# Attention in a decoder layer: scores recomputed with keys as weights, value matmuls with 64-column weights

## The reference

```python
smask = (kpos <= t)                       # keys of the 8 chosen 64-key blocks of each query and group
s_s = einsum('bqgrd,bgqkd->bqgrk', qb, ksel)
p_s = masked_softmax(s_s, smask)          # exp(s - max) * mask / sum
o_s = einsum('bqgrk,bgqkd->bqgrd', p_s, vsel)
wmask = (wpos >= 0) & (diff >= 0) & (diff < WINDOW)       # the last 512 keys
s_w = einsum('bqgrd,bkgd->bqgrk', qb, kwin)
p_w = masked_softmax(s_w, wmask)
o_w = einsum('bqgrk,bkgd->bqgrd', p_w, vwin)
out = g[..., 0:1] * o_cmp + g[..., 1:2] * o_sel + g[..., 2:3] * o_win
```

## Time and profile before

| | us |
|---|---|
| median of 3 runs | 1602.13 |
| lowest and highest of them | 1602.12, 1605.62 |
| the profiled execution | 1602.32 |
| its span, first to last instruction | 1600.5 |
| busy in the span: PE, PEld | 1407.8, 868.7 |
| busy in the span: DVE, ACT, POOL | 564.3, 398.4, 203.1 |

### The profile page before, as it was taken

The page is one execution under the profiler, slowest core; times in us unless marked ns, Lnnn a source line. Parts: engine busy times, 40 slices in busy tenths (PEclk is TensorE's granted clock), DMA queues, the critical chain, the costliest instruction groups (busy, mean ns, idle before and its releaser), DMA issues. The chain is left out here.

```text
span 1600.5 us, 16935 instructions
## 1 busy us (share of the span) xinstructions
PE 1407.8 (88%) x6098; PEld 868.7 (54%) x6118; DVE 564.3 (35%) x1130; ACT 398.4 (25%) x974; POOL 203.1 (13%) x250
## 2 busy tenths in 40 slices
PE   6999999999866699999995799998549999999980
PEld 2555555555445587888874455655424444444430
DVE  1323432234363357555452122444531111111115
ACT  1111111111115445544441122323101111111110
POOL 1121211122110021110000000000011111111104
PEclk9999999999987669999997999999669999999995
DMA  9311100112086211100503001110518999999938
GB/s 367 103 38 53 53 27 27 53 40 66 1 296 237 74 33 42 39 2 27 224 7 122 27 27 40 53 40 27 180 57 278 372 368 371 372 366 371 368 136 315
DMA packets 126916, 227.96 MB, mean 142 GB/s; under 512 B 6272, under 2 KB 82304, under 8 KB 126720
## 3 DMA queue, kind: packets, MB, share of 16 engines
q1 hardware_dynamic: 118640, 197.17, 35.1%
q0 software_dynamic: 7056, 25.69, 4.2%
q10 hardware_dynamic: 1152, 4.19, 0.8%
HBM read 185.09 MB, written 41.94 MB: 142 GB/s over the span
## 5 line engine op out<-in xcount | busy, mean ns | idle before, releaser
L437 PE MATMUL pj<-arena,xT 128*128 128x512 f32 (+1 forms) x768 | 315.3, 564 | 15.2 <-DMA gcol<-in_gcol 15.2
L1719 PE MATMUL egu<-arena,exT 128*128 128x512 f32 x512 | 228.1, 599 | 1.2 <-issue 1.2
L437 PEld LDWEIGHTS pj<-arena,xT 128*128 128x128 f32 x768 | 143.3, 191 | 156.7 <-issue 136.3
L1719 PEld LDWEIGHTS egu<-arena,exT 128*128 128x128 f32 x512 | 95.8, 192 | 110.7 <-issue 110.2
L1118 DVE TENSOR_REDUCE anm<-asc 128x1 f32<-128x640 f32 (+7 forms) x128 | 90.6, 708 | 124.1 <-PE asc L1022 123.4
L1079 ACT ACTIVATE ap<-asc,anm 128x640 f32<-128x640 f32 (+7 forms) x128 | 89.8, 701 | 159.6 <-DVE anm L1118 149.3
L1707 PE MATMUL eyp<-arena,ehT 128*128 128x512 f32 x256 | 115.2, 593 | 1.1 <-ACT ehT L1750 1.1
L1277 PE MATMUL xpj<-arena,xTA 128*128 128x512 f32 x256 | 112.8, 599 | 0.7 <-ACT xTA L1344 0.7
L228 ACT ACTIVATE raw<-pj,xr 128x512 f32<-128x512 f32 (+1 forms) x48 | 31.4, 655 | 300.0 <-PE pj L437 300.0
L1777 DVE TENSOR_TENSOR eh<-esg,egu 128x256 f32<-128x256 f32 x32 | 13.5, 421 | 220.7 <-ACT esg L1756 220.7
L1033 PE MATMUL atp<-early,ap 128*128 128x128 f32 x528 | 84.5, 285 | 5.1 <-ACT apT L1090 4.4
(11 more groups left out here) (317 smaller groups left out, 1940.5 us busy)
## 6 DMA issues: line engine op xcount, KB each, us to landing
arena<-in_w_gate SPq DMA_DIRECT2D x32, 1024.0 KB, 7.4
arena<-in_w_up SPq DMA_DIRECT2D x32, 1024.0 KB, 9.7
arena<-in_w_down SPq DMA_DIRECT2D x32, 1024.0 KB, 11.5
y_d<-ey SPq DMA_DIRECT2D x32, 512.0 KB, 9.6
arena<-in_w_in SPq DMA_DIRECT2D x6, 2048.0 KB, 18.2
y_d<-arena SPq DMA_DIRECT2D x2, 4096.0 KB, 18.6
x<-in_x ACTq DMA_DIRECT2D x8, 512.0 KB, 3.8
xT<-in_xT SPq DMA_DIRECT2D x8, 512.0 KB, 4.0
```

The costliest lines, as they stand in the source:

```text
L437: last = nc.tensor.matmul(dst[:, 0:n], xT[i % 2][:, k, :], w[c][:, k, :], start=k == 0, stop=k == KT - 1)
L1719: last = nc.tensor.matmul(gu[k % 2][:], xT[k % 2][:, c, :], m.gateup[k][:, c, :], start=c == 0, stop=c == KT - 1)
```

## The change

Scores are computed twice. First, only with the high part of the query and in the old orientation, for the maximum of each query, head and branch (`maximum` on TensorE, 192 pieces of at most 512 keys, two PSUM banks; VectorE reduces each). The negated maxima, and the choice of blocks, are transposed once per tile (`turn_shift`), spread over four heads in bf16 (`spread`, `shift`), and later added to the scores by a matmul with constant rows (`m.chosen`, `m.plain`), which also carries the mask of unchosen blocks.

Then the work goes by slots: `attention_slots` gives tile, branch, key tile b and group g, 132 in all. A slot's scores have the key tile as the weight and the group's four heads by 128 queries as 512 moving columns (high, low, causal or window mask if it has one, shift). They land transposed, so ScalarE's exponential writes what the value matmul needs; there are no transposes and copies of probabilities. `values` takes the two slots of a pair, with 64 columns of V as the weight and the 512 probabilities as the moving operand; group 0 goes to partitions 0 to 63 and group 1 to 64 to 127 of one bank. Denominators: GpSimd adds the key tiles' probabilities elementwise (`add`, 100 of 128x512), and `denominators` sums over partitions with matmuls whose weight is a shifted unit column. `keep` and `turn_back` bring result and denominators back to one query per partition.

The maxima of tile i+1 are spread over the slots of tile i (`share`); those of tile 0 come before the first slot. ScalarE makes the high parts, GpSimd the low ones, three buffers each, and SyncE loads the first three tiles' queries at once. The spare stores now stand ahead of the store of tile 7. `phase_select` loads 1 MB of constant rows ahead of the output weights and keeps `m.notsel`.

```diff
+def attention_slots():
+    for i in range(NT):
+        for branch, k0, n in ((0, 0, i + 1), (1, max(0, i - 4), min(i + 1, 5))):
+            for b in range(n):
+                for g in range(NG):
+                    yield i, branch, k0, b, n, g
...
@@ phase_select, sync
+                sp.dma_start(m.tail[:, 0:2 * S + 2], io["chosen"]).then_inc(s["rows_in"], 16)
                 sp.dma_start(m.w_out, io["w_out"].rearrange("(k p) n -> p k n", p=P)).then_inc(m.w_out_in, 16)
...
@@ phase_attend
+    DEN, KEEP, BACK, GATE = 2, 3, 3, 4
+    at_pair = lambda j, lag: [x for x in range(X) if last_pair[x] + lag == j]
+    def share(n):
+        i = slots[n][0]
+        k, total = n - first_slot[i], first_slot[i + 1] - first_slot[i]
+        if i + 1 == NT:
+            return range(0), False
+        use, count = max(1, total - 2), len(pieces[i + 1])
+        return range(count * min(k, use) // use, count * min(k + 1, use) // use), k == total - 1
...
@@ sync
+                for i in range(3):
+                    load_q(i)
+                load_oc(0)
+                load_oc(1)
                 for i in range(NT):
+                    if i + 3 < NT:
+                        load_q(i + 3)
                     if i == NT - 1:
                         sp.wait_ge(m.w_out_in, 48)
...
                             sp.dma_start(spare[b], m.w_out).then_inc(s["spare"], 16)
-                store(NT - 2)
-                store(NT - 1)
+                    store(i)
+                    if i + 2 < NT:
+                        load_oc(i + 2)
...
@@ tensor
+                def maximum(i, p):
...
+                    if f >= 2:
+                        pe.wait_ge(s["read"], f - 1)
...
+                    last = nc.tensor.matmul(dst[:, 0:n * P], qhi[i % 3][:, h, :], kT[:, g, (k0 + c) * P:(k0 + c + n) * P],
+                                            start=True, stop=not masks and not chosen)
...
+                def scores(n):
...
+                    if n >= 2:
+                        pe.wait_ge(s["expd"], n - 1)
+                    keys = (m.kwT if branch else m.ksT)[:, g, (k0 + b) * P:(k0 + b + 1) * P]
+                    dst = sT[n % 2]
+                    for j, q in enumerate((qhi, qlo)):
+                        nc.tensor.matmul(dst[:], keys, q[i % 3][:, 4 * g:4 * g + 4, :].rearrange("p h q -> p (h q)"),
+                                         start=j == 0, stop=False)
+                    for at, mask in marks_of(i, branch, k0, b, 1, nb):
+                        nc.tensor.matmul(dst[:], mask[:], bc(m.identb[:].unsqueeze(1), [P, 4, P]), start=False, stop=False)
...
+                    nc.tensor.matmul(dst[:], keep, shift[i % 2],
+                                     start=False, stop=True).then_inc(s["scored"], 1)
...
+                def values(j):
...
+                    for g in range(NG):
+                        at = (k0 + b) * P + g * HD
+                        last = nc.tensor.matmul(ov[branch][g * HD:(g + 1) * HD, :], v[:, at:at + HD], target(2 * j + g),
+                                                start=b == 0, stop=b == nb - 1)
...
+                def denominators(x):
...
+                    for r in range(HPG):
+                        for g in range(NG):
+                            last = nc.tensor.matmul(dn[g * HD:(g + 1) * HD, 0:P], unit[:, HPG - 1 - r:HPG - 1 - r + HD],
+                                                    acc[x % 2][g][:, r * P:(r + 1) * P], start=r == 0, stop=r == HPG - 1)
...
+                pe.wait_ge(s["ready"], 2)
+                for p in range(len(pieces[0])):
+                    maximum(0, p)
+                turn_shift(0)
+                for j in range(J + BACK):
+                    if j < J:
+                        for n in (2 * j, 2 * j + 1):
+                            scores(n)
+                            some, turning = share(n)
+                            for p in some:
+                                maximum(slots[n][0] + 1, p)
+                            if turning:
+                                turn_shift(slots[n][0] + 1)
+                    if 1 <= j <= J:
+                        values(j - 1)
+                    for x in at_pair(j, BACK):
+                        turn_back(x)
+                    for x in at_pair(j, DEN):
+                        denominators(x)
...
@@ scalar
+                    nc.scalar.activation(target(n), sT[n % 2][:], ACT.Exp).then_inc(s["expd"], 1)
...
@@ gpsimd
+                    a = acc[branch][g][:]
+                    nc.gpsimd.tensor_tensor(a, a, target(n), ALU.add).then_inc(s["summed"], 1)
```

More of the change, by code:

```diff
@@ L1037, in values @@
[L1037 to L1046 removed]
+                    dst = mx[f % 2]
+                    masks = marks_of(i, branch, k0, c, n, total)
@@ new lines, in maximum, with turn_shift @@
+                    for j, (at, mask) in enumerate(masks):
+                        last = nc.tensor.matmul(dst[:, at * P:(at + 1) * P], m.identb[:], mask[:], start=False,
+                                                stop=j == len(masks) - 1)
+                    last.then_inc(s["top"], 1)
+                def turn_shift(i):
+                    f = turn_of[i]
+                    pe.wait_ge(s["wide"], i + 1)
+                    pe.wait_ge(s["read"], f - 1)
+                    nc.tensor.transpose(mx[f % 2][:, 0:P], m.tail[:, 2048:2048 + P],
+                                        m.c("ident")).then_inc(s["top"], 1)
@@ new lines, in keep @@
+                def keep(x):
+                    act.wait_ge(s["denned"], x + 1)
+                    if x >= 2:
+                        act.wait_ge(s["turned"], x - 1)
+                    nc.scalar.activation(oT[x % 2], ov[x % 2][:], ACT.Copy).then_inc(s["kept"], 1)
+                    nc.scalar.activation(dT[x % 2], dn[:, 0:P], ACT.Copy).then_inc(s["kept"], 1)
+                for i in range(3):
+                    high(i)
+                for n in range(U + 2 * KEEP):
+                    if n % 2:
+                        for x in at_pair(n // 2, KEEP):
+                            keep(x)
+                    if n >= U:
+                        continue
+                    exponentials(n)
+                    i = slots[n][0]
+                    if n == (first_slot[i] + first_slot[i + 1]) // 2 and 3 <= i + 2 < NT:
+                        high(i + 2)
@@ L1169, in _ @@
[L1169 to L1178 removed]
+                nc.vector.memset(wide, 0.0).then_inc(s["ready"], 1)
@@ new lines, in _ @@
+                done(nc.vector.memset(unit[:], 0.0))
+                nc.vector.memset(unit[:, HPG - 1:HPG], 1.0).then_inc(s["ready"], 1)
+                dve.wait_ge(s["ready"], 2)
+                for p in range(len(pieces[0])):
+                    maximum(0, p)
+                widen(0)
+                spread(0)
+                for j in range(J + GATE + STEPS + 1):
+                    for n in (2 * j, 2 * j + 1):
+                        if n < U:
+                            i = slots[n][0] + 1
+                            some, turning = share(n)
+                            for p in some:
+                                maximum(i, p)
+                                if p == len(pieces[i]) - 1:
+                                    widen(i)
+                            if turning:
+                                spread(i)
+                        if n == 2 * j:
+                            for i, k in steps_at(j):
+                                finish(i, k)
+                            for x in at_pair(j, GATE):
+                                if x >= 2:
+                                    gate(x)
+                    for x in at_pair(j, BACK):
+                        if x < 2:
+                            gate(x)
```

374 lines of the change are left out of this document (199 added, 175 removed).

## The result

The changed kernel takes 1610.78 us (median of 20 runs, 1604.52 to 1617.79) against 1603.60 us (median of 20, 1600.46 to 1614.35) of the kernel before on the same chip: a ratio of 1.0038, 95% interval 1.0022 to 1.0053, some 6.1 us slower (the two medians alone lie 7.2 apart). Forecast was 1600, 1.9 us faster than before, in a range of 1594 to 1608. The profiled execution took 1614.64 us (span 1612.7). A few executions, whatever the kernel, fall into a second, slower state; the ratios here leave them out.

The account below looks back on a forecast made before the run. TensorE was taken to bound the attention stage (busy 239 of 248 us in its middle). Start +6.3, tile 1 to last values -10.6, end +2.4: -1.9 from 1602.3 gives 1600.4, forecast 1600, range 1594 to 1608.

Parts of the forecast that it names:

- Value pairs, overlap, the price for changing shape: A pair's two value matmuls overlap fully in column halves, 0.85 us, plus 0.33 for changing array shape: 1.2 us.
- Rivals 4 and 5: Value pairs slower: partial overlap, 1.43 us a pair, 1619, chance 0.10; no overlap, 70 us more, 1670, chance 0.05.
- Denominators: TensorE's 16 times 8 matmuls of 128 columns in alternating halves: 1.2 us each time, 19.2 us in all.
- Start: From the selection stage to tile 1's beginning at 577.7 us: a loss of 6.3 us.
- a store's wait behind 1 MB: In the selection stage, the output copy's store waits behind the constants in SyncE's queue: 2.7 us more.
- Tile 0 itself: Attention's first tile: 16 maximum pieces before any slot, 7.7 us, then its slots, three at half clock taking 5.1 us.
- From tile 1 to the last values: TensorE's stretch from 577.7 to 850.6 us: 272.9 us, against 283.5 before, a gain of 10.6.
- 6% waits: TensorE's waiting from tile 1 on, taken at the earlier kernel's share: 15.4 us, between 5 and 31.
- Rival 3: VectorE's reductions pace TensorE in bursts of maxima or behind a finishing step: waits of 31 us, 1616, chance 0.16.
- At most 1.18 each: GpSimd's 100 additions of 128x512: at most 1.18 us each, hidden; from 1.3 us they would pace the last tile.
- End: From the last values to the addition of both branches: 4.3 us, against 1.9 before, a loss of 2.4.
- 8 MB of spare stores: Stores moved behind tile 6 go out about 34 us before the last store, take 18.6 to land: hidden.

Follow-up runs that it names:

- e7: Changed kernel with both value products of a pair in the same column half from tile 1 on; 1651.65 us, one run.
- e6: Kernel before with only the changed kernel's selection stage (1 MB load and GpSimd's copies); 1.0021 of the kernel before.
- e3: Changed kernel with the 1 MB load issued behind the fourth compressed tile's store; 1.0020 of the kernel before.
- e5: Changed kernel with the edits of e1 and e2, and finish steps 5 and 6 one pair later; 0.9987 of the kernel before.
- e9: e5 with the constant rows packed as bf16 pairs and loaded in place, without GpSimd's copies; 0.9964 of the kernel before.
- e10: e9 with GpSimd's additions cut to 8 of 512 columns and the gate's inversion made a copy; 0.9883 of the kernel before.
- e1: Changed kernel with GpSimd taking the power step ahead of the additions of the same pair; 1.0044 of the kernel before.
- e2: Changed kernel with VectorE's gates ahead of its finish steps, and two buffers for the first gated sum; 1.0015 of the kernel before.
- e11: e9 with the whole additions of exponentials on VectorE instead of GpSimd; 0.9985 of the kernel before.
- e4: Changed kernel with GpSimd's additions cut to 8 of 512 columns and the gate's inversion made a copy; 0.9946 of the kernel before.

## Why the prediction was wrong

Point by point, against its own steps:

- **Value pairs, overlap, the price for changing shape.** Right: 1.01 us from the pair's first start to the next line and some 0.1 ahead of it, where 1.2 in all was forecast; e7 confirms 0.85 for the overlap. Rivals 4 and 5 are out. Denominators: 1.09 us for 16 matmuls at full clock, forecast 1.2.
- **Start.** Tile 1 was forecast to begin at 577.7 and begins at 578.95, but 3.74 us of that is scatter from upstream, so the near hit is luck. From the selection's first load on, the start costs 3.8 us more than before in this profile, not 6.3. In it the selection stage has 1.96 (3.4 by e6), where 2.7 were forecast for another reason: a store's wait behind 1 MB. The store's wait did not come, and moving the load (e3) did not help; what fits the profiles is GpSimd's copy. Tile 0 itself costs 1.9 and not 3.6; the clock was at full from 571.0 to 574.4 us, before the end of its slots, and half again until 577.8.
- **From tile 1 to the last values.** Forecast 272.9, of it 256.5 work, 15.4 waits ("I take 6% waits again, 15.4 us") and 1 for the clock. Measured 861.0 - 578.95 = 282.1, so waits and clock are 25.6 instead of 16.4. **This is the step that failed**, by 9.2 us. The work was right: TensorE is busy 259.4 us there, some 3.2 of them lost to half clock. Its waits were mis-sized: they are 22.6 us, and the 7.2 too many are the one wait of 7.0 us for the gate in tile 2, which the forecast did not have. The clock behind it is the other 2.2 (3.2 instead of 1). Without that wait (e5, whose edits aim at it) the kernel is 8.2 us faster.
- **Luck in the rest of it.** Less the 7.0 us the waits are 15.6, the forecast's 15.4 almost to the point. But no wait of the changed kernel had gone into that number, and 13 us of the run hang on additions (e9, e10) that the forecast had as hidden. The share fitted by chance.
- **Why it failed.** The waits were carried over as a share from a kernel whose queues looked different. The text named finishing steps in VectorE's queue, but priced none: neither that the power step (1.65 us) is behind two additions on GpSimd, nor that a gate stands behind a step which waits for it. Rival 3 is nearest: it named a finishing step in the queue among its places, and its mark, more than 20 us of TensorE's idle time put down to VectorE, was met with 21.6 (8.6 + 7.9 + 4.3 + 0.8). But its mechanism was pacing by the reductions, which was 7.9 us only, and its price too high (31 us of waits and 1616, against 22.6 and 1610.8).
- **GpSimd's additions.** "At most 1.18 each" was too low:

```profile
L1234 POOL TENSOR_TENSOR aacc<-aacc,kcvcT 128x512 f32<-128x512 f32 x68 | 89.1, 1329 | 96.0 <-PE aov L1132 73.9 <-ACT kcvcT L1194 21.8
```

  1.33 us is over the 1.3 named as the point where they pace the last tile; they did not (GpSimd 32.87 of 40 us busy, TensorE 39.94). Their cost is of another kind, and the forecast had it at nothing, as hidden: 13 us by e9 and e10.
- **End.** Last values to addition of the branches 865.36 - 861.0 = 4.4, forecast 4.3. From the last store to the next stage's first load it is 3.15 us instead of 2.40. The forecast had the 8 MB of spare stores as hidden, going out 34 us before the last store; they went out 21.7 us before it (850.70 and 872.35 us). The traces show that they hold the next stage: in the changed kernel, e1, e2, e3, e5, e9 and e11 its first load comes 24.7 to 24.9 us behind them, whenever the last store goes, while in e4, e7 and e10, where the last store is 23.4 us or more behind them, the step after it is 2.40 to 2.42 us.

Sum of the profile: +1.96 selection, +1.85 start, -1.4 from tile 1, +2.5 end, +0.5 behind it (from that addition to the next stage's first load 10.1 us, before 9.6), 5.4 us; the runs say 6.1.

The groups of VectorE's operations by shape, 577 to 862 us of the changed kernel, show who is slowed (busy us, mean ns):

```profile
L1291 DVE TENSOR_TENSOR arena<-atp,aw 128x512 f32<-128x512 f32 x15 | 10.4, 692 | 0.5
L1307 DVE TENSOR_TENSOR arena<-arena 128x512 f32<-128x512 f32 x7 | 9.8, 1397 | 0.2
L1290 DVE TENSOR_TENSOR aw<-aw,gate 128x8 f32<-128x8 f32 x15 | 9.0, 597 | 0.5
...
L1311 DVE TENSOR_REDUCE astat<-arena 128x8 f32<-128x512 f32 x7 | 4.7, 678 | 0.1
```

Operations on two tiles in SBUF are slowed (in the mean, L1307 to twice its 0.69 us, L1290 from 0.17 us to 0.60); a product with one input from PSUM (L1291) and a reduction of one tile (L1311) are not. The Trainium skill (SBUF — State Buffer, Who interferes with whom) states this rule: VectorE with two SBUF inputs, or in a two-port mode, and a GpSimd instruction that reads SBUF exclude each other for a whole instruction, and who issues first has it. By that rule, the trace agrees, with the 1.67 us of L895 and these four groups; it would have been a reason to count the additions against VectorE's queue too, and not against GpSimd's alone.

## What to carry to other kernels

Don't carry a share of waits from one kernel to another: list, for each engine's queue, the instruction that waits longest and what stands behind it, above all where two engines hand a small step to and fro (here a power of 128x8 numbers) between large ones. Work moved to an idle GpSimd is not free where VectorE works on pairs of SBUF tiles at the same time: look at VectorE's duration of the same line with and without it, and where it can be had, load tables in the form in which they are used rather than convert them there. When one edit only moves a wait, look for the step that waits in both, and move that.

## What the runs showed of the hardware

- Beside a copy of 2048 columns on GpSimd, an operation of 8 columns on VectorE took 1.67 us instead of 0.17. The eight profiles with this copy have a selection stage 3.4 us longer in the mean than the five without, more than twice the hold itself.
- A wait's length alone does not say whether the clock falls: 2.0 us of idle time at 709.9 us in e9 were followed by a granted clock of 0.65 for 4 us, while in the changed kernel a turn's wait of 2.8 us, up to 725.6 us, was followed by full clock. TensorE had been busy before both.
- Two f32 matmuls of 512 columns with 64-column weights cost 1.01 us together in different column halves, in the same half 1.86 (e7).
- GpSimd's addition of 128x512 takes 1.33 us, more than half of its subtraction of 128x1024 (1.18); VectorE takes 0.71 for it.
